# RWKV preparation and token shift in parts among the last chunks of the input projection, and the forget logits in rounded parts

## What is computed

```python
prev = jnp.pad(p, ((0, 0), (1, 0), (0, 0)))[:, :-1]
p = p + (prev - p) * mu
r, k, v, xw, xa, xg = split_cols(p, RWKV_SPLITS)      # 1024, 1024, 1024, 64, 64, 160
w = -jax.nn.softplus(-(w0 + jnp.tanh(xw) @ w_decay_up)) - 0.5
decay = jnp.exp(-jnp.exp(w))
a = jax.nn.sigmoid(a0 + xa @ a_up)
g = jax.nn.sigmoid(xg) @ g_up
kk = heads(k * k_k); kk = kk / max(norm(kk), 1e-12)
k = k * (1.0 + (a - 1.0) * k_a)
# recurrence over tokens -> y; group norm of y
bonus = sum(r * k * r_k, per head) * v
out = (norm(y) + bonus) * g
```

## Time and profile before

| | |
|---|---|
| median of three runs | 3494.64 us (3486.57 to 3496.1) |
| profiled execution | 3493.31 us, span 3491.6 us |
| granted TensorE clock, mean | 0.871 of full |
| busy: PE, POOL, DVE, ACT | 73%, 74%, 48%, 31% of the span |
| chain that ended last | PE 50%, POOL 23%, DMA 11%, DVE 7%, issue 6%, ACT 2% |

### The profile page before, as it was taken

How to read it: one execution, slowest core, us unless ns; L and a number is a source line. 1 busy time by engine, 2 the same in 40 slices (tenths; PEclk the granted TensorE clock), 3 DMA queues, 4 the chain that set the end, 5 groups by cost and what they waited for, 6 DMA issues and landing times.

```text
span 3491.6 us, 42762 instructions
## 1 busy us (share of the span) xinstructions
PE 2531.9 (73%) x15849; PEld 1985.6 (57%) x15849; DVE 1686.1 (48%) x2277; ACT 1091.1 (31%) x2113; POOL 2582.2 (74%) x1835
## 2 busy tenths in 40 slices
PE   7996778899999999989999899306701750472067
PEld 5884577678998899879898678302300320131023
DVE  4003366424220132231321435897698879788954
ACT  5442423455444444454445655100000000000000
POOL 7897802868999999988675577886687578657852
PEclk9997899999999999999999999758955975786589
DMA  5666400345665666546454354899999999999998
GB/s 177 182 190 161 139 3 3 104 144 163 184 188 189 181 182 191 186 153 175 129 150 121 109 177 151 316 427 427 427 427 427 427 427 427 427 426 427 427 427 346
DMA packets 239894, 868.01 MB, mean 249 GB/s; under 512 B 18594, under 2 KB 20772, under 8 KB 173028
## 3 DMA queue, kind: packets, MB, share of 16 engines
q0 software_dynamic: 73776, 536.97, 36.5%
q1 hardware_dynamic: 163414, 316.11, 29.8%
q10 hardware_dynamic: 2540, 12.75, 1.3%
HBM read 860.24 MB, written 2.10 MB: 247 GB/s over the span
## 4 chain that ended last, share of the span: by engine, by line
PE 50%; POOL 23%; DMA 11%; DVE 7%; issue 6%; ACT 2%; DVEq 0%; POOLq 0%; SPq 0%; ACTq 0%
PE acc L1867 20%; PE acc L1877 19%; DMA zone<-in_peer_v,zone 11%; POOL zone L713 9%; POOL lasting L713 9%; POOL w_lo L597 5%; PE acc L1873 3%; PE acc L1996 3%; PE acc L2422 2%; DVE lasting L1808 1%; PE acc L2311 1%; DVE zone L1417 1%; PE acc L2242 0%; PE acc L1914 0%; DMA lasting<-in_w_mix_out 0%
## 5 line engine op out<-in xcount | busy, mean ns | idle before, releaser
L597 POOL TENSOR_TENSOR w_lo<-lasting,w_hi 128x512 fp32r<-128x512 f32 (+1 forms) x1184 | 1591.6, 1363 | 332.1 <-ACT w_hi L758 307.0
L758 ACT ACTIVATE w_hi<-lasting 128x512 fp32r<-128x512 f32 (+1 forms) x1184 | 742.8, 632 | 925.3 <-PE acc L1867 458.6
L2422 PE MATMUL acc<-zone,lasting 128*128 128x512 f32 x512 | 257.7, 662 | 699.9 <-ACT lasting L1235 639.1
L2422 PEld LDWEIGHTS acc<-zone,lasting 128*128 128x128 f32 x512 | 105.7, 212 | 851.3 <-ACT lasting L1235 498.4
L713 POOL DMA_INDIRECT zone<-in_peer_v,zone x128 | 189.1, 1477 | 177.7 <-DVE lasting L1808 74.7
L1877 PE MATMUL acc<-x_hi,w_hi 128*128 128x256 f32 (+1 forms) x1856 | 305.9, 287 | 16.8 <-DVE x_lo L1546 6.0
L1778 DVE CUSTOM_DVE_ANT_0 zone<-lasting,zone 128x2048 f32<-128x2048 f32 x128 | 293.4, 2292 | 30.4 <-DMA lasting<-in_peer_u,zone 20.3
L1778 DVE CUSTOM_DVE_ANT_0 zone<-zone 128x2048 f32<-128x2048 f32 x128 | 293.4, 2292 | 22.9 <-DMA zone<-in_peer_u,zone 13.6
L1877 PE MATMUL acc<-x_lo,w_hi 128*128 128x256 f32 (+1 forms) x1856 | 299.4, 283 | 0.0
L1877 PE MATMUL acc<-x_hi,w_lo 128*128 128x256 f32 (+1 forms) x1856 | 299.1, 283 | 0.0
L713 POOL DMA_INDIRECT zone<-in_peer_u,zone x128 | 256.2, 2002 | 50.1 <-issue 37.5
(11 more groups left out here) (417 smaller groups left out, 3890.7 us busy)
## 6 DMA issues: line engine op xcount, KB each, us to landing
lasting<-in_w_in SPq DMA_DIRECT2D x200, 512.0 KB, 3.6
lasting<-in_w_up SPq DMA_DIRECT2D x128, 512.0 KB, 3.8
lasting<-in_w_down SPq DMA_DIRECT2D x128, 512.0 KB, 4.3
lasting<-in_w_mix_out SPq DMA_DIRECT2D x32, 512.0 KB, 3.7
lasting<-in_w_out SPq DMA_DIRECT2D x32, 512.0 KB, 3.6
lasting<-in_peer_w_query SPq DMA_DIRECT2D x32, 512.0 KB, 3.6
lasting<-in_w_kv_cross SPq DMA_DIRECT2D x16, 512.0 KB, 3.8
lasting<-in_w_q_cross SPq DMA_DIRECT2D x8, 512.0 KB, 3.6
```

The source lines that it names most:

```text
L597: pool.tensor_tensor(w_lo[:, k, 0:width], ring[:, slot, s % SLOT_SLABS, 0:width], w_hi[:, k, 0:width].bitcast(FP32), ALU.subtract).then_in ...
L758: act.activation(w_hi[:, s % PARTS, 0:width], ring[:, slot, s % SLOT_SLABS, 0:width], ACT.Copy).then_inc(hi_ready, 1)
L2422: last = pe.matmul(bank(4 * t + c), diag[:, n // 2, k], rows_buf[2 * n + k][:, c * CHUNK:(c + 1) * CHUNK], start=hx % 2 == 0 and i == 0 an ...
```

## The change

- `in` and `in_end` become one product of ten chunks, written out without a loop. `at_slabs` places functions by the slab number (0 to 159) in ACT's and PE's queues.
- The shift is done in three parts: r and k (after ACT's slab 36), v (68), LoRA columns (83). `mu` is loaded in four pieces, three after ACT's slab 10 and the last at 83. DVE mixes in operations of 1024 (and 288) columns.
- The preparation's PE parts are placed before slabs 91, 95, 99, 103, 116 and 130, in banks 4 to 7, with buffers of their own for the two token tiles. ACT's parts stand behind its slabs 66 to 139.
- The sums of the squared keys move from POOL to DVE. SP loads four parameter rows before the tiles of chunk 2, and r_k after the last tile.
- POOL rotates queries and keys after the preparation (`s_el`), beside the recurrence. Bonus sums move from DVE to POOL, beside the recurrence. The statistics of y's first token tile are taken after the second group.
- POOL splits `w_logit` into two rounded parts, and PE does the forget logits as 48 rounded products instead of 32 in FP32.

```diff
-        prev = at(Z + TILES * D, TILES, RWKV_COLS)
-        mu = at(Z + TILES * D + TILES * RWKV_COLS, RWKV_COLS)
...
+        logd = [params[:, n] for n in range(TILES)]
+        z_gate = [kk_sq, at(zs, R_W)]
...
+        prev_rk, prev_v, prev_lora = at(Z, TILES, 2 * R_W), at(zs + 4 * R_W, TILES, R_W), at(zs + 4 * R_W, TILES, LORA)
...
-            Product("in", w("w_in"), D, 2 * CHUNK, [CHUNK] * 8, True, 2),
-            Product("in_end", w("w_in"), D, 10 * CHUNK, [CHUNK, IN_COLS - 11 * CHUNK], True, 2),
+            Product("in", w("w_in"), D, 2 * CHUNK, [CHUNK] * 9 + [IN_COLS - 11 * CHUNK], True, 10),
...
+        decay_sum = lambda t: acc[:, 4 + 2 * t:6 + 2 * t].rearrange("p a b -> p (a b)")
+        at_slabs = lambda calls: {divmod(n, SLABS): f for n, f in calls.items()}
...
+            def load_params():
+                chunk_done(sp, G["cross_v"], 0)
...
+                for n, name in enumerate(("a0", "k_k", "k_a")):
+                    sp.dma_start(params[:, n], A[name][0].partition_broadcast(P)).then_inc(s_par, 16)
...
+                        if (g.name, c) == ("in", 2):
+                            load_params()
...
-                if g.name == "in_end":
-                    sp.wait_ge(s_mixed, TILES)
...
-                    sp.dma_start(params[:, 3], A["r_k"][0].rearrange("h n -> (h n)").partition_broadcast(P)).then_inc(s_par, 16)
+                if g.name == "in":
+                    sp.wait_ge(s_gd, TILES)
+                    sp.dma_start(bonus_row, A["r_k"][0].rearrange("h n -> (h n)").partition_broadcast(P)).then_inc(s_par, 16)
...
-            pool.wait_ge(s_par, 16 * 5)
...
-                step(TT(key_t[:, t], p[:, t, R_W:2 * R_W], params[:, 1], ALU.mult))
-                step(TT(kk_sq, key_t[:, t], key_t[:, t], ALU.mult))
-                head_sums(kss[:, t], heads(kk_sq), kk_sq).then_inc(s_kss, 1)
...
             pool.wait_ge(s_trig, 1)
             for k in range(4):
                 pool.wait_ge(acc_free[k], G["mix"].used0[k] + 1)
+            pool.wait_ge(s_el, TILES)
...
-                g_wait(pool, len(PAIRS) - 1, "y", u, 1)
+            pool.wait_ge(s_par, 16 * 5)
+            for t in range(TILES):
+                step(TT(kk_sq, p[:, t, 0:R_W], p[:, t, R_W:2 * R_W], ALU.mult))
+                step(TT(kk_sq, kk_sq, bonus_row, ALU.mult))
+                step(head_sums(bonus[:, t], heads(kk_sq), kk_sq))
...
+                    g_wait(pool, 2 * t + 1, "y", u, 1)
...
+            pool.wait_ge(s_meta, 16)
+            step(pool.tensor_copy(logit_w[0], w_logit))
+            TT(logit_w[1], w_logit, logit_w[0].bitcast(FP32), ALU.subtract).then_inc(s_lw, 1)
...
+            def load_mu():
+                act.dma_start(mu_r, A["rwkv_mu"][0, 0:R_W].partition_broadcast(P)).then_inc(s_shift, 16)
...
+                act.dma_start(mu_v, A["rwkv_mu"][0, 2 * R_W:XW0].partition_broadcast(P)).then_inc(s_shift_v, 16)
+            def shift(dst, col, n, reads, done):
                 for k in range(4):
...
+                    act.wait_ge(acc_free[k], g.used0[k] + 1 + sum(k // 2 == c % 2 for c in range(reads)))
                 for t in range(TILES):
                     for a, b in ((0, 112), (112, P - 1)):
-                        act.dma_start(prev[a + 1:b + 1, t], p[a:b, t, 0:RWKV_COLS]).then_inc(s_shift, 16)
...
+                        act.dma_start(dst[a + 1:b + 1, t], p[a:b, t, col:col + n]).then_inc(done, 16)
+                act.dma_start(dst[0:1, 1], p[P - 1:P, 0, col:col + n]).then_inc(done, 16)
+            def shift_v():
+                act.wait_ge(s_kss, TILES)
+                shift(prev_v, 2 * R_W, R_W, 4, s_shift_v)
+            def shift_lora():
+                act.wait_ge(s_mixed, 3 * TILES)
+                act.dma_start(mu_lora, A["rwkv_mu"][0, XW0:RWKV_COLS].partition_broadcast(P)).then_inc(s_shift_lora, 16)
+                shift(prev_lora, XW0, LORA, 5, s_shift_lora)
+            def load_lora():
+                act.wait_ge(s_mixed, 3 * TILES)
+                act.dma_start(lora_up[0:LORA_W, 0], A["w_decay_up"][0]).then_inc(s_lora, 16)
...
+            def key_roots():
+                act.wait_ge(s_kss, TILES)
+                act.activation(kss, kss, ACT.Sqrt).then_inc(s_ksd, 1)
+            def bend_lora():
+                act.wait_ge(s_mixed, 4 * TILES)
+                for t in range(TILES):
...
+                    act.activation(xw, xw, ACT.Tanh).then_inc(s_tanh, 1)
+                    act.activation(xg, xg, ACT.Sigmoid).then_inc(s_sig, 1)
...
+            def read_gates(t):
+                act.wait_ge(s_gd, t + 1)
...
+            def exp_minus(t):
+                act.wait_ge(s_cp, t + 1)
+                act.activation(z_gate[t], z_gate[t], ACT.Exp).then_inc(s_ea, 1)
+                act.activation(logd[t], decay_sum(t), ACT.Exp, scale=-1.0).then_inc(s_en, 1)
+            def exp_plus(t):
+                act.activation(decayC[:, t], bank(6 - 2 * t)[:, 0:R_HEADS].rearrange("p (g c) -> p g c", c=2), ACT.Exp)
+                act.wait_ge(s_kd, t + 1)
+                act.activation(z_gate[t], decay_sum(t), ACT.Exp).then_inc(s_ep, 1)
...
+                p[:, t, (2 + c) * CHUNK:(2 + c) * CHUNK + g.widths[c]], src, ACT.Copy)), between=at_slabs({
+                    8: sines, 10: load_mu, 36: lambda: shift(prev_rk, 0, 2 * R_W, 2, s_shift), 66: key_roots, 68: shift_v,
+                    72: lambda: act.preload_act_table_set("sigmoid_and_others"), 83: shift_lora, 85: load_lora, 90: bend_lora,
+                    102: lambda: bend_z(0), 104: lambda: bend_z(1), 107: lambda: bend_a(0), 109: lambda: bend_a(1),
+                    112: lambda: read_gates(0), 114: lambda: read_gates(1),
+                    121: lambda: exp_minus(0), 125: lambda: exp_plus(0), 135: lambda: exp_minus(1), 139: lambda: exp_plus(1)}))
...
+            def mix(prev, mu, col, n):
+                for t in range(TILES):
+                    cur = p[:, t, col:col + n]
+                    step(TT(prev[:, t], prev[:, t], cur, ALU.subtract))
+                    step(TT(prev[:, t], prev[:, t], mu, ALU.mult))
+                    TT(cur, cur, prev[:, t], ALU.add).then_inc(s_mixed, 1)
+            step(dve.memset(prev_rk[0:1, 0], 0.0))
+            dve.wait_ge(s_shift, 16 * 7)
+            mix(prev_rk[:, :, 0:R_W], mu_r, 0, R_W)
+            mix(prev_rk[:, :, R_W:2 * R_W], mu_k, R_W, R_W)
+            dve.wait_ge(s_mixed, 2 * TILES)
+            dve.wait_ge(s_par, 16 * 4)
             for t in range(TILES):
...
+                step(TT(key_t[:, t], p[:, t, R_W:2 * R_W], params[:, 1], ALU.mult))
+                step(TT(kk_sq, key_t[:, t], key_t[:, t], ALU.mult))
+                RED(kss[:, t], heads(kk_sq), AX, ALU.add).then_inc(s_kss, 1)
+                dve.wait_ge(s_kss, t + 1)
+            step(dve.memset(prev_v[0:1, 0], 0.0))
+            dve.wait_ge(s_shift_v, 16 * 6)
+            mix(prev_v, mu_v, 2 * R_W, R_W)
+            dve.wait_ge(s_mixed, 3 * TILES)
+            step(dve.memset(prev_lora[0:1, 0], 0.0))
+            dve.wait_ge(s_ksd, 1)
+            step(dve.tensor_scalar_max(kss, kss, 1e-12))
+            step(dve.reciprocal(kss, kss))
+            for t in range(TILES):
+                step(TT(heads(key_t[:, t]), heads(key_t[:, t]), kss[:, t].unsqueeze(2).to_broadcast([P, R_HEADS, R_HEAD]), ALU.mult))
+            dve.wait_ge(s_shift_lora, 16 * 6)
+            mix(prev_lora, mu_lora, XW0, LORA)
             dve.wait_ge(s_lt, 1)
             step(dve.tensor_copy(loraT[:, 0:2], acc[:, 4:6, 0:SEQ]))
             dve.tensor_copy(loraT[0:LORA_G - P, 2], bank(6)[0:LORA_G - P, 0:SEQ]).then_inc(s_lT, 1)
...
-            dve.wait_ge(s_par, 16 * 5)
...
+            for t in range(TILES):
+                dve.wait_ge(s_zd, t + 1)
+                TT(z_gate[t], decay_sum(t), w0, ALU.add).then_inc(s_zv, 1)
+            for t in range(TILES):
+                dve.wait_ge(s_ad, t + 1)
+                TT(beta_t[:, t], decay_sum(t), params[:, 0], ALU.add).then_inc(s_av, 1)
+            dve.wait_ge(s_av, TILES)
+            for t in range(TILES):
+                dve.wait_ge(s_ze, t + 1)
+                dve.tensor_scalar_mul(logd[t], z_gate[t], -E_HALF).then_inc(s_ld, 1)
             for t in range(TILES):
                 r_, k_ = p[:, t, 0:R_W], p[:, t, R_W:2 * R_W]
...
+                a_, kk, tmp = beta_t[:, t], key_t[:, t], z_gate[t]
                 dve.wait_ge(s_ae, t + 1)
                 dve.wait_ge(s_ld, t + 1)
                 step(STT(tmp, a_, -1.0, params[:, 2], ALU.add, ALU.mult))
...
                 step(STT(k_, tmp, 1.0, k_, ALU.add, ALU.mult))
-                step(TT(tmp, r_, k_, ALU.mult))
-                step(TT(tmp, tmp, params[:, 3], ALU.mult))
-                step(RED(bonus[:, t], heads(tmp), AX, ALU.add))
...
                 step(TT(a_, a_, kk, ALU.mult))
                 dve.wait_ge(s_cd, t + 1)
...
+                TT(tmp, decay_sum(t), logd[t], ALU.subtract).then_inc(s_cp, 1)
+                dve.wait_ge(s_ea, t + 1)
                 dve.wait_ge(s_en, t + 1)
```

(38 more changed lines are left out.)

172 lines of the change are left out of this document (56 added, 116 removed).

## The result

| | before | changed |
|---|---|---|
| median | 3491.9 us (4 runs, 3486.6 to 3496.1) | 3439.0 us (4 runs, 3433.3 to 3442.1) |
| ratio, 95% interval | | 0.9846 (0.9828 to 0.9864) |
| profiled execution | 3493.3 us | 3442.1 us |
| recurrence starts | 449.64 us | 408.80 us |

What follows compares the result with a forecast made beforehand. The first block's projection and preparation hold 101.5 us that are not projection; 67.2 come back, gaining 34.3, plus 0.7 behind it and 8.9 in the logits: 43.9 faster, forecast 3451 us, range 3427 to 3477.

Steps and rivals of the forecast that it cites:

- rival A: Everything fits: ACT's blocks fall into POOL's slow stretches, more contention behind PE's products; 3429 us, chance 0.13.
- (1): PE's small preparation products, placed before slabs inside the projection, are paid in full: 24.9 us added, bounds 22 to 35.
- (2): In the projection, two-SBUF-operand DVE operations beside POOL cost 0.84 us each; 26.5 us after hiding 9, bounds 15 to 48.
- rival B: Contention is dear: each DVE operation's whole 1.29 us is lost and nothing hides; 3477 us, chance 0.13.
- (3): ACT's blocks in the projection cost 2.3, 3.5 and 4.5 us plus 4 of waits: 14.3 us, bounds 3 to 35.
- (4): Shift transfers delay weight tiles in the projection, but the ring of eight slabs covers it: 0 us, bounds 0 and 8.
- (5): At the projection's end, ACT's reads of the last chunk and PE's waits cost 1.5 us.
- (6): Behind the projection: POOL beside the recurrence +3 us, PE entering warm -1.7, statistics out of index scores -2; sum -0.7.
- (7): Forget logits as 48 rounded products take 6.1 instead of 15.0 us: gain 8.9, bounds 7 and 10; POOL's split 0.
- Rivals C: Shift handovers are late, so ACT stops rounding at slabs 67, 84 and 91, 7 us each; 3472 us, chance 0.14.
- D: Slower: PE's clock stays at 1.2 GHz from slab 36 to 141; 144 us more, 3595 us, chance 0.03.
- E: The preparation's chain still ends after the projection and the recurrence waits for it; 3485 us, chance 0.03.

Runs made afterwards that it cites:

- e5: Changed kernel with the gate's 8 FP32 products of 512 columns cut to two of 16, gate left out of the result; median 3436.1 us in two runs.
- e3: Changed kernel with 24 unread DVE operations added beside the projection's first slabs, 12 two-SBUF-operand multiplications and 12 tensor-scalars; median 3450.7 us.
- e6: Changed kernel with POOL's bonus sums computed four times per token tile instead of once; median 3461.0 us.
- e8: Changed kernel with parameter rows one chunk later, r, k and v shift transfers one per slab, and DVE's key operations beside PE's stops; median 3426.9 us.
- e9: e8 with the shift and mix of r split off and started 14 slabs earlier; median 3427.8 us.
- e11: Changed kernel with POOL's bonus sums set to zero, so the bonus is left out of the result; median 3438.6 us.
- e2: Changed kernel with the ten transfers of the shifts of r, k and of v issued one per slab, sigmoid table load at slab 74; median 3439.2 us.
- e1: Changed kernel with the four parameter rows (2 MB on SP's queue) loaded one chunk later; median 3439.3 us.
- e10: Changed kernel with the second tile's decay product and the ACT exponentials behind it 12 slabs later; recurrence starts 3.8 us later, no median given.

## Why the prediction was right, and where its parts were not

The time, 3439.0, lies 12 us under the forecast and inside the range; it also is 1 us below the forecast's own range (3440 to 3462), so a small share of rival A is in it. 51.3 measured against 43.9 is 7.4 us: 5.1 in the preparation, 2.2 more behind it (forecast 0.7 gained, measured 2.9), 0.2 in the logits, 1.6 from POOL's split, 1.4 at the very start, and -3.1 of clock at other places.

(1) **Small products** 24.9: measured 23.6. The decay sums were 0.9 cheaper, and the six transposes took 0.7, not 1.4: I had taken their price from a group at the lower clock. e5 shows the gate's part paid in full.

(2) **DVE beside POOL** 26.5: measured 24.3 (10.6 + 4.6 + 9.1). The price of 0.84 was right to the hundredth (e3), which rules out rival B. Hidden were 11 us, not 9, and not where I put it: I gave the lead to PE's small products alone, but ACT's blocks make one too. The 288-column operations, 2.2 in my sum, cost next to nothing. The Trainium skill's page "SBUF — State Buffer" (section "SBUF: two separate sides") says that the one of the two engines that comes second is blocked for the other's whole instruction. The traces agree, if the rule is read as turns: beside a stream of POOL's 512-column operations a 1024-column operation of DVE takes 2.2 us instead of 1.23, so it loses some 1.0 us to one of them, and POOL is held once per operation. In e6, where POOL's operation is the longer one (2.4 us), DVE's of 0.29 us took 2.42. The length that counts is that of the other engine's operation.

(3) **ACT's blocks** 14.3: measured 12.2 in the first two, about 1 at the third. The sum came out by luck, with errors of both signs. The step "the first block (no table load) costs 2.3" failed: 8.0, since the issue took 8.4 us and PE restarted at half clock. The third's 4.5 and the 4 of waits were together near 1: ACT's wait of 3.7 for the LoRA mix is there, and of it PE stood 0.77 us for a late slab of POOL behind the transposes (285.38).

(4) **DMA stall** 0: right for the changed kernel, by cover only. The block of ACT stood in front of it: with the block spread, 2.9 us of late weight tiles appeared (e8), and half the bytes removed them (e9).

(5), (6), (7): end 1.1 to 1.5 as put. The recurrence gained 1.4 where I had +1.7 and -3: of the 3 for POOL the bonus sums cost 0.4 (e11), and all of DVE's operations together are 0.6 us longer than before (78.63 against 78.04). Index scores 1.5 for 2. Logits 9.0 for 8.9. POOL's two small operations ahead of the second block, put at 0, gained 1.6: they kept POOL's rounding off DVE's first two operations. That gain was not looked for.

Rivals C, D and E fell: one wait of 3.7 us instead of three of 7; clock 0.98; DVE done 24.8 us ahead of PE.

## What to carry to other kernels

When a buffer of a few tiles stands between a slow producer (POOL) and a fast consumer (PE), price a stop of the consumer and the contention of the producer together: the first 2 to 3 us of contention after a stop were free here, so put the operations that disturb the producer beside and right behind stops that must be there, and expect little from removing a stop alone (e2: 2.1 of 9.3 us) until that is done (e8: 10.2 in the slabs). Two short operations ahead of a burst on POOL can pay when DVE's waited-for operations stand there (1.6 us for 0.9 of work). Beside a serial chain on DVE, look at the length of POOL's operations, and at which of the chain's own read two SBUF operands. Read a change place by place: where identical instructions differ by 2 to 5 us with the clock, the end time of one run doesn't tell 4 us from nothing.

## What the runs showed of the hardware that I had not expected

- Five SBUF-to-SBUF issues on ACT's queue took 8.4 us for 2.1 MB (DMA share 0.92), 5.2 for 1.0 MB, and some 4.3 for 3.4 MB in the kernel before (share 0.98 from 266.2 to 270.5). It is not the bytes alone, and what else it is stays open: moving 2 MB of rows away from it (e1) took off 0.6 us.
- After the same stop of 7.2 us, PE went through the second block's first slab at a granted clock of 1.00 in the changed kernel (2.42 us) and of 0.51 in e10 (4.40 us), with the same instructions.
- A tensor-scalar operation of 1024 columns goes from 0.69 to 1.70 us beside POOL, but lengthens POOL's slab by only 0.31 (e3).
- A two-pass product of 32 rows takes as long as one of 128 (gate: 1.12 us for either).
